# A backbone step on one Trainium2 core: seven block products a pair also for the mix's gate tiles of m = 1 to 7

## The reference, cut to what matters

```python
def mixer(h, p, ctx):
    z = h @ p['w_in']            # last 3 x 1024 columns: zgate, three branch gates
    ...
    y_a = f @ p['w_o_fourier']
    y_b = attend(q_att, k, v) @ p['w_o_mla']
    y_c = o_g @ p['w_o_gla']
    g = sigmoid(zgate).reshape(B, L, 3, D_MODEL)
    merged = g[:, :, 0] * y_a + g[:, :, 1] * y_b + g[:, :, 2] * y_c
    return merged @ p['w_out'], ...

def layer(x, cond, p, ctx):
    mod = silu(cond) @ p['w_mod'] + p['b_mod']   # shift1, scale1, gate1, shift2, scale2, gate2
    h = rms_norm(x, norm1_g) * (1 + scale1) + shift1
    x = x + gate1 * mixer(h, p, ctx)
    h2 = rms_norm(x, norm2_g) * (1 + scale2) + shift2
    return x + gate2 * (square(relu(h2 @ w_ff1)) @ w_ff2)
```

## Time and profile before

| | before |
|---|---|
| runs | 2080.69, 2082.92, 2084.91 us, median 2082.92 |
| profiled execution | 2083.18 us, its span 2081.4 us (1.8 us lie around the span) |
| PE busy | 2008.2 us, 96% of the span |
| DVE, ACT, POOL busy | 53%, 42%, 8% |
| mean granted TensorE clock | 0.992 of full |
| HBM read | 187.79 MB, 93 GB/s |

### The profile page before, as it was taken

The page is one execution under the profiler, slowest core; times in us unless marked ns, Lnnn a source line. Parts: engine busy times, 40 slices in busy tenths (PEclk is TensorE's granted clock), DMA queues, the critical chain, the costliest instruction groups (busy, mean ns, idle before and its releaser), DMA issues.

```text
span 2081.4 us, 33810 instructions
## 1 busy us (share of the span) xinstructions
PE 2008.2 (96%) x14192; PEld 1840.9 (88%) x14192; DVE 1095.8 (53%) x1939; ACT 879.6 (42%) x1634; POOL 159.6 (8%) x141
## 2 busy tenths in 40 slices
PE   6999999999999999999999999999999999999997
PEld 3985688989989999999989866888899899999997
DVE  4245686333464573645553466953335655646464
ACT  5525544222354262534455355442223643535262
POOL 0000000000000030403100000000000002121210
PEclk9999999999999999999999999999999999999999
DMA  9210011453214424232532100114532221313131
GB/s 364 73 51 11 1 36 42 171 195 124 78 51 157 148 72 142 92 124 100 167 108 73 34 9 1 47 58 175 195 111 73 70 71 61 102 61 102 62 92 61
DMA packets 53032, 195.92 MB, mean 94 GB/s; under 512 B 6032, under 2 KB 8144, under 8 KB 52112
## 3 DMA queue, kind: packets, MB, share of 16 engines
q1 hardware_dynamic: 49408, 174.61, 24.9%
q0 software_dynamic: 3472, 19.14, 2.4%
HBM read 187.79 MB, written 5.93 MB: 93 GB/s over the span
## 4 chain that ended last, share of the span: by engine, by line
PE 86%; DVE 8%; ACT 3%; DMA 2%; issue 2%; SPq 0%; DVEq 0%; ACTq 0%
PE ps L661 50%; PE ps L818 14%; PE ps L838 2%; PE ps L728 2%; PE ps L984 2%; PE ps L847 2%; PE ps L679 2%; PE ps L766 2%; PE ps L960 2%; PE ps L1014 2%; PE ps L989 1%; DVE w_lo_parts L1599 1%; DVE scratch L1997 1%; ACT scratch L1429 1%; DMA w_raw<-in_stream 1%
## 5 line engine op out<-in xcount | busy, mean ns | idle before, releaser
L1599 DVE TENSOR_TENSOR w_lo_parts<-w_raw,w_hi_parts 128x512 fp32r<-128x512 f32 x512 | 373.5, 759 | 399.9 <-ACT w_hi_parts L1186 344.1
L1186 ACT CAST w_hi_parts<-w_raw 128x512 fp32r<-128x512 f32 x344 | 195.9, 618 | 526.9 <-PE ps L661 517.8
L661 PE MATMUL ps<-h_hi_parts,w_hi_parts 128*128 128x320 f32 x1216 | 280.8, 312 | 2.3 <-DVE h_lo_parts L1599 2.3
L661 PE MATMUL ps<-hid_hi_parts,w_hi_parts 128*128 128x320 f32 x1216 | 279.3, 311 | 0.0
L661 PE MATMUL ps<-hid_lo_parts,w_hi_parts 128*128 128x320 f32 x1216 | 277.1, 309 | 0.0
L661 PE MATMUL ps<-h_hi_parts,w_lo_parts 128*128 128x320 f32 x1216 | 277.1, 309 | 0.0
L661 PE MATMUL ps<-h_lo_parts,w_hi_parts 128*128 128x320 f32 x1216 | 277.0, 309 | 0.0
L661 PE MATMUL ps<-hid_hi_parts,w_lo_parts 128*128 128x320 f32 x1216 | 277.0, 309 | 0.0
L1787 DVE SCALAR_TENSOR_TENSOR x<-ps,modulation,x 128x128 f32<-128x128 f32 (+2 forms) x216 | 81.7, 434 | 290.8 <-PE ps L661 290.8
L661 PEld LDWEIGHTS ps<-h_hi_parts,w_hi_parts 128*128 128x128 f32 x1216 | 202.5, 188 | 21.1 <-issue 17.6
L661 PEld LDWEIGHTS ps<-hid_hi_parts,w_hi_parts 128*128 128x128 f32 x1216 | 202.2, 188 | 16.8 <-issue 16.8
(11 more groups left out here) (296 smaller groups left out, 3487.1 us busy)
## 6 DMA issues: line engine op xcount, KB each, us to landing
w_raw<-in_stream SPq DMA_DIRECT2D x312, 512.0 KB, 3.7
scratch<-in_first SPq DMA_DIRECT2D x10, 512.0 KB, 13.9
small_weights<-in_small POOLq DMA_DIRECT2D x2, 2048.0 KB, 11.0
h_scratch<-in_first SPq DMA_DIRECT2D x6, 512.0 KB, 17.0
x<-in_xT POOLq DMA_DIRECT2D x2, 1280.0 KB, 11.4
x<-in_xT POOLq DMA_DIRECT2D x8, 320.0 KB, 4.5
x_kept<-x POOLq DMA_DIRECT2D x8, 320.0 KB, 3.1
x<-x_kept POOLq DMA_DIRECT2D x8, 320.0 KB, 4.6
```

The costliest lines, as they stand in the source:

```text
L661: ins = mm(pair(o)[:, h, :], w[:, s % 2, k, :], a[:, k, h * HALF:(h + 1) * HALF], start=(first and n == 0), stop=(last and n == 2))
L1186: copy(wh[:, s % SPLIT, ks, :], raw[:, t % RAW, ks, :]).then_inc(w_hi, 1)
L1599: return tt(dst, full, hi.bitcast(F32), ALU.subtract)
```

## The change

In the mix, the pairs (G1_m, G2_m) of m = 1 to 7 are made by seven block products; m = 0 and the feed-forward's block 0 stay whole. Parts of it:
- `mods_after`: the pairs follow the products of G1_m for all m and of G2_0 (9 in each layer), of O0 to O4 in layer 0 or O0 to O2 in layer 1, and of FF1 and FF2 in layer 0; those of the later blocks stay.
- The differences of h for the mix are made at its start: DVE puts h together again in four quarters (`quarter_in_full`), then in m = 0 four differences, ACT four casts, DVE four low parts (in place).
- The ring of split weights is counted in half tiles over the whole kernel (`ENTRIES`, `RING`), entry r taking the place of entry r-4; `cast_entry` and `low_entry` serve whole tiles and blocks.
- DVE's five sums of a pair write the two gate pre-activations to `G`; ACT takes each sigmoid in place, in two instructions behind the pair, with its own semaphore `mix_sig`. The second branch product moves to banks 2 and 3, the first and third to banks 4 and 5.
- POOL makes four block sums for each m before it reloads x[:, m]; x[:, 0] comes last, since a modulation row is kept there.
- In the feed-forward, block 0's `full_h`, differences, casts and low parts come earlier (with the products of FF0 to FF4), and the banks of a pair are 0, 1, 2, 3 or 4, 5, 2, 3.

The core of the diff:

```diff
@@ mods_after
-    if MIX0 + 3 <= i < MIX0 + 15:
+    if MIX0 <= i < OUT0:
+        m, q = divmod(i - MIX0, 3)
+        return int(q == 0 or (m, q) == (0, 1))
+    if OUT0 <= i < OUT0 + (5 if l == 0 else 3):
         return 1
-    if l == 0 and FF0 + 1 <= i < FF0 + 5:
+    if l == 0 and FF0 + 1 <= i < FF0 + 3:
         return 1
@@ by_sevens, ring_entries
+    i = s % PER
+    if MIX0 <= i < OUT0:
+        m, q = divmod(i - MIX0, 3)
+        return m >= 1 and q < 2
+def ring_entries():
+    out = []
+    for s in range(MAIN):
+        if leads(s):
+            out += [(s, n, False) for n in range(SEVEN)]
+        elif not by_sevens(s):
+            out += [(s, n, True) for n in range(2)]
+    return out
@@ gpsimd
+                for m in range(1, KT):
+                    block_sums(e.layer * PER + MIX0 + 3 * m)
                     pool.wait_ge(gate_used, e.at(gate_used, m + 1))
                     pool.dma_start(x[:, m, :], src[:, m, :]).then_inc(x_back[m], 16)
@@ tensor, the mix
+                    if m > 0:
+                        pair_by_sevens(o, i, {0: o - 5, 2: o - 2})
+                    for q in range(2 if m == 0 else 0):
                         tile_ready(i + q)
                         banks_read(o + q)
-                        product(o + q, i + q, hh, hl)
+                        product(pair(o + q), i + q, hh, hl)
+                        pe.wait_ge(og_rstd, e.at(og_rstd, 1))
                         modulation(i + q)
...
+                        product(branch_banks(b), i + 2, uh, ul, ks)
@@ tensor, pair_by_sevens
+                    pe.wait_ge(block_lo, b + n + 1)
+                    if n in (2, 3, 4, 6):
+                        pe.wait_ge(diff_ready, e.at(diff_ready, (0 if mix else 4) + {2: 1, 3: 2, 4: 3, 6: 4}[n]))
@@ scalar
+            def cast_entry(r):
+                s, n, whole = ENTRIES[r]
+                if n == 0 or not whole and n == 6:
+                    t = PLACE["main", s + (n == 6)]
+                    act.wait_ge(raw_in[t % RAW], 16 * (t // RAW + 1))
+                if r >= 4:
+                    old, c, was_whole = ENTRIES[r - 4]
+                    if was_whole:
+                        act.wait_ge(mm_done, product_of(old, c))
+                    else:
+                        act.wait_ge(block_mm, BLOCK[old] + c + 1)
...
+            def pair_step(s, n):
+                if n in (0, 2, 4):
+                    act.wait_ge(block_mm, BLOCK[s] + n + 1)
+                    if n == 4:
+                        act.wait_ge(p57_sb, BLOCK[s] // SEVEN + 1)
+                    copy(copies(s)[n // 2], ps[:, block_bank(s, n), 0:HALF]).then_inc(ready, 1)
+                cast_entry(RING[s] + n + 4)
@@ scalar, the mix
                     fn(G[:, 0, :], x[:, m, :], ACT.Sigmoid).then_inc(gate_used, 1)
...
+                        for n in range(2 * q, 2 * q + 2):
+                            cast_diff(True, n)
+                    if m > 0:
+                        for n in range(SEVEN):
+                            pair_step(e.layer * PER + i, n)
+                        for q in range(2):
+                            act.wait_ge(pair_free[(o + q) % 2], ...)
+                            fn(G[:, 1 + q, :], G[:, 1 + q, :], ACT.Sigmoid).then_inc(mix_sig, 1)
@@ scalar, feed-forward block 0
-                        if q == 2:
+                        if q == 0:
                             act.wait_ge(h_ready, e.at(h_ready, 4 * KT))
-                        if 2 <= q < 6:
-                            full_h(q - 2)
+                        if q < 2:
+                            full_h(2 * q)
+                            full_h(2 * q + 1)
+                        elif q < 4:
+                            cast_diff(False, 2 * q - 4)
+                            cast_diff(False, 2 * q - 3)
@@ vector
+            def quarter_in_full(n):
+                ins = tt(diff(True, n), quarter(hh, *QUARTER[n]).bitcast(F32), quarter(hl, *QUARTER[n]).bitcast(F32), ALU.add)
+                if n == 3:
+                    e.link(ins)
@@ vector, the mix
+                for n in range(4):
+                    quarter_in_full(n)
                 for m in range(KT):
                     i, o = MIX0 + 3 * m, O_MIX + 5 * m
-                    for q in range(2):
+                    for q in range(2 if m == 0 else 0):
+                        make_diff(True, 2 * q)
+                        make_diff(True, 2 * q + 1)
                         split_next(i + q)
                         modulation(i + q)
+                    if m > 0:
+                        for n in range(SEVEN):
+                            pair_step(e.layer * PER + i, o, n, (G[:, 1, :], G[:, 2, :]))
...
                         tt(dst, branch_banks(b), halves(G[:, b, :]), ALU.mult).then_inc(pair_free[r % 2], 1)
+                        if b > 0:
+                            low_entry(RING[e.layer * PER + i + 2] + 3 + b)
...
+                        if m == 0:
+                            for n in ((0, 1), (2,), (3,))[b]:
+                                low_diff(True, n)
```

More of the change, by code:

```diff
@@ L160, in product_of @@
         m, q = divmod(i - MIX0, 3)
-        n = done(O_MIX + 5 * m + (q if q < 2 else 4))
+        n = done(O_MIX + 5 * m + (q if q < 2 else 3 + half))
     else:
@@ L865, in _ @@
                     banks_read(q)
-                    product(q, q, hh, hl)
+                    product(pair(q), q, hh, hl)
                     modulation(q)
@@ L1154, in _ @@
                             banks_read(o + q)
-                            product(o + q, i + q, hh, hl)
+                            product(pair(o + q), i + q, hh, hl)
                         modulation(i + q)
+                    for q in range(0, KT, 2) if f > 0 else ():
+                        n = o + q
+                        first = q == 0
+                        pair_by_sevens(n, i + q, {0: n - 2, 2: n - 1} if first else {0: n - 4, 2: n - 2, 3: n - 1})
                     for q in range(KT if f < FF_BLOCKS - 1 else KT - 2):
@@ new lines, in cast_entry @@
+                s, n, whole = ENTRIES[r]
[8 more added lines that the diff above has]
+                        act.wait_ge(block_mm, BLOCK[old] + c + 1)
+                if whole:
+                    copy(place(wh, r), raw_half(s, n)).then_inc(w_hi, 1)
+                    return
@@ L1217, in hid_by_sevens, with split_next @@
+                if 2 <= n < 6:
+                    act.wait_ge(block_sum, 4 * BLOCK[s] // SEVEN + n - 1)
+                copy(place(wh, r), block_source(s, n)).then_inc(block_hi, 1)
+            def split_next(i):
+                for n in range(2):
+                    cast_entry(RING[e.layer * PER + i] + 4 + n)
             def hid_by_sevens(f, q, o):
@@ L1345, in _ @@
             norm_factor()
-            split_hi(0)
+            for r in range(2):
+                cast_entry(r)
             unit_row(1)
-            split_hi(1)
+            for r in range(2, 4):
+                cast_entry(r)
             first_norm()
@@ L1623, in low_block, with split_next @@
                     return
-                j, n = divmod(g, SEVEN)
-                dve.wait_ge(block_hi, e.at(block_hi, (f - 1) * PAIR_BLOCKS + g + 1))
-                low(block_place(wl, g), block_source(s + 2 * j, n), block_place(wh, g)).then_inc(block_lo, 1)
+                dve.wait_ge(block_hi, BLOCK[s] + n + 1)
+                low(place(wl, r), block_source(s, n), place(wh, r)).then_inc(block_lo, 1)
+            def split_next(i):
+                for n in range(2):
+                    low_entry(RING[e.layer * PER + i] + 4 + n)
             def hid_low(f, q):
@@ L1655, in pair_by_sevens @@
                         dve.wait_ge(hid_sq, e.at(hid_sq, KT * f + q))
[L1656 to L1657 removed]
+                    pair_step(e.layer * PER + FF0 + 2 * KT * f + q, o + q, n, (gqk[:, 0, :], gqk[:, 1, :]))
+                    if n == 0 and not first:
                         hid_low(f, q - 2)
[L1659 removed]
+                    if n == 2 and not first:
                         hid_low(f, q - 1)
[L1662 to L1664 removed]
+            def quarter_in_full(n):
+                ins = tt(diff(True, n), quarter(hh, *QUARTER[n]).bitcast(F32), quarter(hl, *QUARTER[n]).bitcast(F32), ALU.add)
+                if n == 3:
+                    e.link(ins)
@@ L1670, in make_diff, with low_diff @@
                 tt(dst, a, b, ALU.subtract).then_inc(diff_sum, 1)
+            def low_diff(mix, n):
+                dve.wait_ge(diff_cast, e.at(diff_cast, (0 if mix else 4) + n + 1))
+                low(diff_lo(mix, n), diff(mix, n), diff_hi(mix, n)).then_inc(diff_ready, 1)
             def unit_read(u):
@@ L1801, in _ @@
                 hat(0, 1, k).then_inc(first_hat, 1)
-            for s in range(SPLIT):
-                split_lo(s)
+            for r in range(4):
+                low_entry(r)
             unit_read(1)
```

414 lines of the change are left out of this document (197 added, 217 removed).

## The result

The changed kernel takes 2103.74 us (median of four executions, 2099.59 to 2108.52) against 2082.57 us: ratio 1.0102, 95% interval 1.0074 to 1.013, so 21.2 us slower. Forecast were 2096.6 us. The profiled execution took 2106.7 us, its span is 2104.5 us, 23.1 more than before; all rows of after are from this one.

The account below looks back on a forecast made before the run. PE, at work 96% of the span, was taken to bound the kernel. Terms: -27.3 + 22.8 + 4.8 + 10.0 + 3.4 = +13.7 us, from 2082.9 to 2096.6; range 2077 to 2112, the forecast's own 2087 to 2106.

Parts of the forecast that it names:

- What is removed: Whole kernel: 24.6 us of matmuls, 1.8 of modulation waits and 0.9 at the output's start go, together 27.3 us.
- The 0.9 at the start of the output: Output start: DVE has two low parts less, so the wait falls from 1.15 to 0.7 us a layer, 0.9 in all.
- m = 0: Mix start: late tile at G2_0's pair (8.8 us), clock fall (1.9), then DVE's pace; 11.4 us a layer, 22.8 added.
- the one meeting of 1.3 us: DVE's work for m = 1: one block low part meets a POOL sum, taken as 1.3 us.
- m = 1: Mix: B_1 and its modulation pair go out late, behind the sixth low part; 2.4 us a layer, 4.8 added.
- m = 2 to 7: Later mix pairs: DVE has 11.1 us of work in 20.5, no waits; nothing added, 1 us a pair as upper end.
- The second rival: Every pair late: POOL's sums shut out DVE's low parts in m = 2 to 7; 2109 to 2115 us, chance 0.15.
- its row: Earlier trace: a block's low part that met a POOL sum took 1.78 us, read as lasting until the sum's end.
- Output: O1's modulation pair waits a whole tile landing (3.7 us median), plus the clock's fall; 5.0 us a layer, 10.0 added.
- Feed-forward block 0: Layer 0: FF3's later low parts delay the pair behind FF2 by 2.9 us, 3.4 with some clock; layer 1 none.
- The first rival: Only the wait at G2_0's pair is real, DVE catches up; 2073 us, decided by waits below 23 us; chance 0.13.
- the third: All waits at their low ends, 25.3 us added against 27.3 removed: no change, 2081 to 2087 us; chance 0.14.

Follow-up runs that it names:

- the last comparison: Kernel before, whole products everywhere, with the modulation pair places of the 2059.3 us run: 2080.46 us, 21.2 or 22.0 us above that run, which has 144 matmuls fewer.
- the kernel with both pairs moved: Changed kernel with each layer's modulation pairs behind G2_0 and O1 moved to other places, such as behind B_7: 2077.18 us.
- the best order tried with all seven: Changed kernel with the modulation pairs behind G2_0 and O1, and layer 0's behind FF2, moved elsewhere; all 14 block pairs kept: 2073.93 us.
- DVE's first order: Block pairs from m = 2, most difference work queued behind B_1's low parts, layer 0's FF2 modulation pair moved behind O5; against the kernel before: 2080.41 us.

## Why the prediction was right in sign and 7 us short

- **What is removed.** The 24.6 us hold, by the last comparison (21.2 to 22.0 for 144). The 0.9 at the start of the output don't: the wait was 0.70 us as forecast in layer 0 but 1.51 in layer 1, against 2.3 in two before, 0.1 less in all.
- **m = 0.** The wait was 8.78 and 8.85 us; forecast 8.8 from DVE's queue, a landing and the ring. From G1_0's start to m = 1's fifth block it took 42.3 us (354.79; the first block at 390.07, and four blocks of 1.76), forecast 41.9. The total is right, its two parts not: at half clock the first branch product ended at 384.8 and not at 383.3, and from there DVE needed 12.0 us to the end of the fifth low part, at 396.7, and not 13.1. POOL's four sums ran from 380.5 to 386.0, while DVE was mostly idle, so the one meeting of 1.3 us that the forecast took didn't come. That the two errors cancel is luck. PE hardly waited for the fifth low part, 0.25 us in layer 1, where the forecast looked for 1 to 2 us of such waits.
- **m = 1.** The waits at the modulation pair were 1.52 and 3.48 us, together 5.0; forecast were 2 x 2.4.
- **m = 2 to 7.** No waits, as forecast. The second rival's mechanism exists (above: 2.59 for 1.44), but DVE has slack there: from 430 to 530 it is busy 57.9 of 100 us. The forecast's reading of its row was a little off: the low part of the earlier trace rows ended at 738.74, which is 0.55 us behind the sum's end at 738.19 and not with it, so it ran its own time once the sum was over.
- **Output.** The waits were 3.80 and 3.90 us, forecast 3.7. The stage without its modulation pairs grew by 12.8 - 6.0 = 6.8 and 9.8 - 3.6 = 6.2 us; forecast 5.0 each. The clock cost 3.0 and 2.3 us, not 1.3. This is the term of the sum that was mis-sized: "the clock's fall behind it (1.7 us for 3.4 at half, taken with 0.8)".
- **Feed-forward block 0.** FF2's wait was 2.79 us, forecast 2.9. In layer 1 the forecast's "Layer 1 has no pair there" left out that PE waits for the late low parts themselves, 0.63 and 0.58 us.
- **Stretches that the change doesn't touch.** +0.5, +1.3 and +3.0 us, forecast nothing. The windows of after and, at the same place, of the kernel with both pairs moved show the 3.0 us:

```profile
1380.00:1384.00 4.00, 4.00 (x28) 2.96 (x28) 0.00 (x0) 2.34 (x4) 0.00 (x0) 0.73 0.00 0
1384.00:1388.00 4.00, 4.00 (x22) 2.88 (x20) 0.00 (x0) 0.00 (x0) 0.00 (x0) 0.50 0.00 0
```

```profile
1371.00:1375.00 4.00, 4.00 (x36) 2.84 (x35) 0.00 (x0) 1.55 (x3) 0.00 (x0) 1.00 0.00 0
1375.00:1379.00 4.00, 4.00 (x33) 3.12 (x32) 0.21 (x1) 0.15 (x1) 0.00 (x0) 1.00 0.02 4
```

The wait ahead of this stretch is the same in both (1.37 and 1.38 us), the clock isn't. Four executions of the changed kernel had mean clocks of 0.983, 0.986, 0.980 and 0.986 and took 2106.7, 2099.6, 2108.5 and 2100.8 us: the slower, the lower the clock.

Added up for the profiled execution, with 1.19 us for each modulation pair that a stretch gained or lost:

| stretch | the forecast's terms | sum | measured |
|---|---|---|---|
| both mixes | -24.6 - 1.8 - 0.9 + 22.8 + 4.8, six pairs fewer (-7.1) | -6.8 | -7.2 |
| both outputs | 10.0, eight pairs more (+9.5) | 19.5 | 22.6 |
| norm and block 0 | 3.4, two pairs fewer (-2.4) | 1.0 | 3.0 |
| untouched stretches | none | 0 | 4.8 |

The measured column is 9.5 above the forecast's; 23.1 less 13.7 is 9.4. Of the waits the forecast had 32.7 us for the seven pairs and 33.1 came. So the mechanism was right, and the miss is the clock (and 1.2 us of block 0). PE's busy time says so too: it is 15.1 us above what the matmuls taken away leave, and the forecast's terms hold 6.9 us of clock (2 x 1.9, 2 x 1.3 and 0.5). Why the clock falls in some executions and places and not in others after equal waits stays open.

The first rival (covered after all) fell by its own mark: the waits were not below 23 us. Its thought, that only G2_0's wait is real, is wrong, since O1's alone was worth 15 us. The second needed waits in m = 2 to 7 and the third only 25.3 us added in all, where some 46 came.

## What to carry to other kernels

Where tiles pass through an in-order ring, work out for each added tile which tile had its place and which instruction lets go of it; a tile behind the next two products can need an instruction that isn't reached yet. When a late transfer is taken away, ask what the same late instruction holds up next: here 8.8 us were removed and 3.8 came back for the same low parts. New preparatory work belongs where its engine idles, found in that engine's timeline, and to make the room it can pay to give up a part of the gain: one of seven tile pairs given up in each layer (3.5 us of matmuls in the two layers) brought, once DVE's order was right, 2059.3 us, where the best order tried with all seven reached 2073.9. With DVE's first order the same gift was no gain (2080.4).
